# Two-block network on one core: where the column sums of the second layer's scale stand

## The reference, cut to what matters

```python
def ada_modulate(x, c, norm_g, ada_w, ada_b):
    ada = jax.nn.silu(c) @ ada_w + ada_b
    shift, scale, gate = jnp.split(ada, 3, axis=-1)
    h = rmsnorm(x, norm_g) * (1.0 + scale[:, None, :]) + shift[:, None, :]
    return h, gate[:, None, :]

def even_layer(...):
    h, gate_res = ada_modulate(x, c, norm_g, ada_w, ada_b)
    a, u, v, gate = _split(h @ in_w, EVEN_SIZES)
    ...
    y = jnp.concatenate([ya, yb], axis=-1) * jax.nn.silu(gate)
    return x + gate_res * (y @ out_w)

def odd_layer(...):
    h, gate_res = ada_modulate(x, c, norm_g, ada_w, ada_b)
    gq, gk, gv, glr, sq, sk, sv, gate = _split(h @ in_w, ODD_SIZES)
    ...
```

## Time and profile before

| What | us |
|---|---|
| median of 3 runs (996.51 to 998.18) | 996.55 |
| the profiled execution's own time | 997.37 |
| its span, first to last instruction | 995.5 |
| TensorE busy in the span | 968.9 (97%) |
| VectorE busy | 645.5 (65%) |
| ScalarE busy | 515.8 (52%) |

### The profile page before, as it was taken

One profiled execution on the slowest core, in us unless ns is written; L12 is line 12 of the kernel. 1 busy time (PEld: TensorE's weight loads), 2 busy tenths in 40 slices (PEclk: granted clock), 3 DMA queues, 4 the chain that ended last, 5 costly groups with the idle time before them and its releaser, 6 DMA issues.

```text
span 995.5 us, 19887 instructions
## 1 busy us (share of the span) xinstructions
PE 968.9 (97%) x8833; PEld 936.9 (94%) x8833; DVE 645.5 (65%) x750; ACT 515.8 (52%) x602; POOL 1.1 (0%) x12
## 2 busy tenths in 40 slices
PE   7999999999999999999999999999979999999998
PEld 6899999989999998999899999899879999999998
DVE  3887887763776555664699765355656666466565
ACT  3345454346534578843683542367645654354445
POOL 0000000000000000000000000000000000000000
PEclk9999999999999999999999999999999999999999
DMA  9999548845576444485434432134325366555521
GB/s 340 366 366 310 168 155 270 296 130 170 165 259 212 128 127 128 156 261 165 126 108 144 148 92 86 43 109 146 96 64 190 110 209 212 176 189 192 184 87 43
DMA packets 153442, 172.36 MB, mean 173 GB/s; under 512 B 4001, under 2 KB 137693, under 8 KB 153229
## 3 DMA queue, kind: packets, MB, share of 16 engines
q1 hardware_dynamic: 151696, 167.43, 51.8%
q10 hardware_dynamic: 1660, 3.67, 1.1%
HBM read 170.03 MB, written 1.05 MB: 172 GB/s over the span
## 4 chain that ended last, share of the span: by engine, by line
PE 48%; DVE 7%; ACT 4%; issue 2%; DVEq 0%
PE pj L2500 36%; DVE w_lo L1365 2%; ACT w_hi L896 1%; PE m_all L2225 1%; PE m_all L2227 1%; PE m_all L2214 1%; PE pj L2459 1%; PE pj L2461 1%; PE pj L2460 1%; PE pj L2316 1%; PE m_all L2350 1%; DVE work L1759 0%; PE m_all L1932 0%; PE m_all L2377 0%; PE m_all L1984 0%
## 5 line engine op out<-in xcount | busy, mean ns | idle before, releaser
L1365 DVE TENSOR_TENSOR w_lo<-raw,w_hi 128x2048 fp32r<-128x2048 f32 (+2 forms) x128 | 288.0, 2253 | 154.0 <-ACT w_hi L896 153.2
L2500 PE MATMUL pj<-h_hi,w_hi 128*128 128x256 f32 x1232 | 351.3, 285 | 6.1 <-DVE h_lo L1768 3.0
L2500 PE MATMUL pj<-h_hi,w_lo 128*128 128x256 f32 x1232 | 345.2, 280 | 0.0
L2500 PE MATMUL pj<-h_lo,w_hi 128*128 128x256 f32 x1232 | 345.1, 280 | 0.0
L896 ACT ACTIVATE w_hi<-raw 128x2048 fp32r<-128x2048 f32 (+2 forms) x128 | 239.9, 1876 | 100.9 <-PE pj L2500 69.1
L2500 PEld LDWEIGHTS pj<-h_hi,w_hi 128*128 128x128 f32 x1232 | 231.3, 188 | 13.8 <-issue 9.0
L2500 PEld LDWEIGHTS pj<-h_lo,w_hi 128*128 128x128 f32 x1232 | 231.4, 188 | 0.3
L2500 PEld LDWEIGHTS pj<-h_hi,w_lo 128*128 128x128 f32 x1232 | 231.1, 188 | 0.2
L2500 PE MATMUL pj<-y_hi,w_hi 128*128 128x256 f32 x600 | 169.1, 282 | 1.9 <-DVE y_lo L1852 1.9
L2500 PE MATMUL pj<-y_hi,w_lo 128*128 128x256 f32 x600 | 167.8, 280 | 0.0
L2500 PE MATMUL pj<-y_lo,w_hi 128*128 128x256 f32 x600 | 167.6, 279 | 0.0
(11 more groups left out here) (380 smaller groups left out, 1187.7 us busy)
## 6 DMA issues: line engine op xcount, KB each, us to landing
raw<-in_odd_in_w_dram SPq DMA_DIRECT2D x28, 1024.0 KB, 5.3
raw<-in_w_in_dram SPq DMA_DIRECT2D x23, 1024.0 KB, 5.3
raw<-in_ada_w_dram SPq DMA_DIRECT2D x22, 1024.0 KB, 7.8
raw<-in_w_ff_in_dram SPq DMA_DIRECT2D x16, 1024.0 KB, 5.4
raw<-in_w_ff_out_dram SPq DMA_DIRECT2D x16, 1024.0 KB, 5.1
raw<-in_even_in_w_dram SPq DMA_DIRECT2D x13, 1024.0 KB, 5.2
raw<-in_even_out_w_dram SPq DMA_DIRECT2D x8, 1024.0 KB, 5.8
raw<-in_odd_out_w_dram SPq DMA_DIRECT2D x8, 1024.0 KB, 5.2
```

Of the source, the lines that this page charges most:

```text
L1365: V.tensor_tensor(w_lo[:, i % SPL, 0:n], raw_of(u)[:, 0:n], w_hi[:, i % SPL, 0:n].bitcast(F32), ALU.subtract).then_inc(S(f"split{i % SPL}" ...
L2500: m = nc.tensor.matmul(to, a_, b_, start=(s == 0 and q == 0 and (fb == 0 or not together)), stop=(s == len(steps_) - 1 and q == 2), skip_g ...
```

## The change

The units n = 17, 18 and 19 are put in the schedule by `ada_sum`, so that DVE's part stays where it was. TensorE's part for n = 17 and n = 19 (entries 0 and 2 of `gate_units`) is put behind `eo` 3, ahead of `ada_rest` and `norm` 1. `gate_units` is emptied, so that the last four units keep their numbers. The entry "norm1" of `keep_busy` is gone.

```diff
-BUSY = {"norm1": (8, 2), "ffn": (8, 2), "gate": (7, 2)}
+BUSY = {"ffn": (8, 2), "gate": (7, 2)}
...
         if i < 3:
-            ada(*later_ada.pop(0))
+            ada_sum(*later_ada.pop(0))
+    scale_units = gate_units[0:3:2]
+    del gate_units[:]
+    for u in scale_units:
+        schedule.append(("ada_out", u))
     step("ada_rest")
...
     step("norm", 1)
-    step("keep_busy", "norm1")
     for i in range(2):
         odd("gk", "copy", 512, i)
```

## The result

| | before | changed |
|---|---|---|
| median of 10 runs, us | 996.77 (996.51 to 998.18) | 999.37 (998.95 to 1000.28) |
| profiled execution, us | 997.37 | 1000.28 |
| its span, us | 995.5 | 998.5 |

The ratio is 1.0023, 95% interval 1.0014 to 1.0033: slower by 2.3 us, within 1.4 and 3.3. The time lies inside the forecast's range, on the side that it named, but beyond the 0.2% under which it had put 74% of the chance, and 1.6 us above its 997.8.

A forecast was written before the change was run, and what follows sets the result against it. TensorE was taken as the bound, busy 968.9 of 995.5 us. Order +0.89 and clock +0.4 made 998.7 from the profiled 997.37, or 997.8 (996.55 + 1.3) on the median's scale; range 996.4 to 999.6.

The forecast's parts named there:

- The bound: Whole kernel: TensorE works 968.9 of 995.5 us, so nearly every microsecond added or taken ahead of a wait counts.
- the seams of `eo` 1 and `eo` 3: Removing the sums gains 0.0 us ahead of `eo` 1, which waits for `w_lo`, and 0.89 us ahead of `eo` 3.
- 0.0 - 0.89 + 1.78 = +0.89: Order's total at the root's start: nothing ahead of `eo` 1, a gain ahead of `eo` 3, all sums paid before `sum_squares`.
- The seam of `eo` 1 and `eo` 2: The chain of weights sets the start of `eo` 2, so any gain ahead of `eo` 1 would be gone: 0.0 us.
- The norm: Behind `eo` 3, ahead of `sum_squares`: both groups of sums are paid, +1.78 us; the later wait of `ada_rest` is hidden, 0.0.
- Rival 3: Sums hidden in front of `sum_squares` while TensorE waits there for ACT's squares: 996.1 us; chance 0.06.
- The floor for small matmuls: For the moved sums: starts about 25 ns apart would make four extra sums cost 0.1 to 0.2 us; the trace disagreed.
- The clock: Pause ahead of `gk` 0: without the products of constants TensorE idles 4.0 us and the clock falls to 0.50, costing 0.4.
- rival 1: The clock stays up at `gk` 0, so only the order's 0.89 us is paid: 997.4 us; chance 0.15.
- I take 0.4, the one stretch: At `gk` 0: one slow stretch of some 3.3 us from the first matmul leaves 3.5 matmuls late, 0.4 us.
- The prediction's own count: Matmuls of `gk` 0 let through by a slow stretch: 0.0 us if begun in the pause, 0.8 at the second chunk.
- Rival 2: Column sums beside the pause starve the clock too, over `sum_squares` or late in `gk` 0: 999.5 us; chance 0.20.

The follow-up runs named there:

- e4: Kernel before with only the column sums of n = 17 moved behind `eo` 3, products of constants kept: ratio 1.0009.
- e8: Kernel before with the column sums of n = 17 done twice at their place in front of `eo` 1: ratio 1.0000.
- e3: Kernel before with only the column sums of n = 19 moved behind `eo` 3, products of constants kept: ratio 1.0004.
- e1: Changed kernel with the eight products of constants put back behind the sum of squares: ratio 1.0009.
- e12: Changed kernel run a third time, unchanged: 998.67 us in a single execution, beside 997.09 for one of the kernel before.
- e2: Kernel before without the eight products of constants, the column sums where they were: ratio 1.0017.
- e9: Kernel before without the eight products of constants, column sums in place, run once more: ratio 1.0010.
- e10: Changed kernel run again, unchanged: ratio 1.0022.
- e7: Changed kernel with four products of constants put in the pause ahead of `gk` 0: ratio 1.0011.
- e6: Kernel before with the column sums of n = 17 and n = 19 moved behind `sum_squares`, into the pause, products of constants kept: ratio 1.0001.
- e5: Kernel before with only the column sums of n = 19 moved behind `sum_squares`, into the pause, products of constants kept: ratio 0.9991.
- e11: Kernel before with only n = 19's column sums moved into the pause, products of constants kept, run once more: ratio 0.9993.

## Why the prediction was right, and where it was off

**The bound, and the seams of `eo` 1 and `eo` 3: right.** With the sums gone `eo` 1 waits for its `w_lo`, with 1.23 us between its loads in the change and in e4, and it starts 0.06 or 0.07 us behind the split's end in every profile but e8's. The sums behind `eo` 2 were paid (e3: no gain or loss from moving them). "0.0 - 0.89 + 1.78 = +0.89" measured 0.85 in the first profile, 0.86 in e4, both at the pace of before, and 1.0009 in the times of e1 and e4.

**The seam of `eo` 1 and `eo` 2: not needed.** I took it as a second reason that a gain would not last. The change's weight loads run on there without a wait, but as `eo` 1 started no earlier, nothing tested it. It had been read from one execution, and it does not hold for all: the split for `eo` 2 ends 13.50 us behind the start of the one for `eo` 1 in the profile of before, but 13.04 in the change's and 12.41 in e12's, so part of a gain could have lasted there.

**The norm: right.** The sixteen sum rows took 1.71 us where I had 1.78, `sum_squares` followed without a gap, and `ada_rest`'s new wait, 0.68 us, was hidden. Rival 3, the sums hidden, falls.

**The floor for small matmuls.** The Trainium skill ("TensorE: Matmul & The Clock Gate", section "Wait — 56ns, not 53.3ns?") puts it at about 25 ns. That did not price these products either when sixteen of their rows stood one behind the other: 0.11 us each (e8).

**The clock: the mechanism right, its size too small.** The fall came in every profile without the products, so rival 1 falls. The term "I take 0.4, the one stretch" is the one that was off. One stretch cost 0.50 to 0.67: the level changed 0.6 to 1.2 us into `gk` 0 in four of the five, and the later it began the more it cost, as more of it lies where the operands no longer set the pace. The prediction's own count, done again for a start at the second chunk, gives 0.6 to 0.7 and not its 0.8: some 21.5 matmuls are through after 4.2 us, where 26.7 would be. Two stretches in a row cost 1.10 and not 2.0, because 2.0 of their 6.8 us lay in the pause; the same count gives 1.1 for the 4.9 us that are left. The Trainium skill ("TensorE: Matmul & The Clock Gate", section "What's actually happening"), read strictly, had left the fall to how the pause lies. Here it came five times of five.

**What stays open.** By the profiles the terms are 0.85 at like pace and 0.69 in the mean, 1.5 together. The times say 2.2 and 2.3, with intervals that reach down to 1.3 and 1.4; and e2 and e9 say 1.7 and 1.0 for the clock alone. The part above the profiles' sum, some 0.7 us, lies within the measurement's uncertainty. If it is real, long falls are more frequent than one in five.

The record bears on that with the mean granted clock of every timed execution, to three decimals. From it the time at half clock can be estimated: a mean of 0.998 over 996 us is about 4 us. With the eight products that gives 3.0 to 5.1 us in the mean of each kernel's executions, 3.2 to 4.1 for the kernel before. Without them it gives 8.9 (e10), 9.4 (e9), 10.0 (e2, but for one execution with a mean of 0.946) and 12.8 (the change): at least 5.7 more than the kernel before beside it, where the five falls at the pause last 4.1 in the mean and one stretch 3.4. So the clock was probably at half for longer in the timed executions than the profiles show. Where is not shown, and the times do not follow it closely: the change and e10, one program, have 12.8 and 8.9 at nearly the same loss. e7, with four products, has 8.0 against 4.1 for the kernel before beside it. That is about one stretch more, though its profile has none at the pause, so four products may not hold the clock as eight do.

Rival 2 had put a second stretch at 20% and gave 999.5. The time came close to that number, but in four of five profiles not by that mechanism: luck, as far as the profiles show.

**The chances.** The forecast's 1.3 us stood only 0.7 below the bound of 2.0, and the clock's term had been read from one stretch at another place, with 0.4 as its value and 0.8 as its upper end. With the 0.5 to 1.1 that the profiles show, the sum is 1.4 to 2.0, and slower was nearer to an even chance than to 0.23. The range's lower end had a slip of its own: 996.4 was to be where the hidden sums lie, and rival 3 puts them at 996.1.

**A better version.** Leave n = 17's sums in their wait, put only n = 19's into the pause, and keep the products: 0.9991 and 0.9993 in two measurements, intervals 0.9982 to 1.0000 and 0.9984 to 1.0002. Its profiles both show 0.44 us gained at the slower pace of `eo`, which is a little under 0.8 at like pace. The times, 0.9 and 0.6 to 0.7 us, fit that, but neither interval alone excludes no gain clearly.

## What to carry to other kernels

Before moving work off a seam of a busy engine, compare the same work at two seams: where the next start follows a supplier's end by a constant 0.06 us, the work is free. Moving it cost its full length at both places tried: 0.86 us behind `eo` 3 (e4), and about 0.9 in the pause (e6 against e5 at like pace). "In front of the norm" and "in the pause of the norm" are different places: the pause begins behind the last product that the root waits for. Work that covers nothing may still hold the clock: an empty pause of 4.0 us cost 0.5 to 1.1 us behind it each time it was profiled. And two traces of one program can differ by as much as the effect: look for a place where the edit changes nothing, here the 288 loads of `eo`, and see whether it took the same time in both.

## What the runs showed of the hardware that was not expected

The slow stretches of the clock at other places come and go between executions of programs that are the same there. At about 731 to 737 the profiles of before, the change, e4, e5, e8, e9, e10 and e12 have one, those of e1, e2, e3, e6, e7 and e11 have none; e1, e7 and e11 have one at about 499; the change and e7, e11 and e12 have one at about 10 to 14, in the start. And TensorE's pace at a granted clock of 1.00 has two values in `eo`, about 117 and 118 ns a step, in executions of one program; nothing here shows why. Together with the start's own drift this moves one execution by about 1 us, as much as either term of this change. So for effects of this size a distance inside the trace, between two marks that the change brackets, says more than the span, as long as the pace between them is the same.
